# Attention steps reordered to scores, transposes, filler, transposes, values, with each head's maximum and exponentials as steps of their own

## The reference

```python
# layer 0: neighbourhood attention, 8 heads of 64, one row of the grid
s_lat = einsum('bhqd,bhiwd->bhqiw', q_r, k_blk) * scale + bias      # NEG outside of the neighbourhood
s_ctx = einsum('bhqd,bhcd->bhqc', q_r, kc) * scale
p = softmax(concatenate([s_lat, s_ctx]))
out = p_lat @ v_blk + p_ctx @ vc
# layer 1: sliding-window attention, 8 heads of 64, window 128, context keys and a sink logit per head
p = softmax(concatenate([s_lat, s_ctx, s_sink]))
out = p[..., :span] @ v_w + p[..., span:span + n_ctx] @ vc
# both: out = merge(out) * silu(gate projection)
```

## Time and profile before

| | |
|---|---|
| median of 3 runs | 1734.81 us (1733.99 to 1734.95) |
| the profiled execution | 1734.62 us |
| its span, first to last instruction | 1732.7 us |
| mean granted TensorE clock | 0.976 of 2.4 GHz |
| TensorE (PE) busy | 1624.4 us, 94% |
| VectorE (DVE) / ScalarE (ACT) / GpSimd (POOL) busy | 671.8 / 549.1 / 36.8 us |
| attention of layer 0 | about 335 to 790 us |
| attention of layer 1 | about 1380 to 1592 us |

### The profile page before, as it was taken

One profiled execution on the slowest core, in us unless ns is written; L12 is line 12 of the kernel. 1 busy time (PEld: TensorE's weight loads), 2 busy tenths in 40 slices (PEclk: granted clock), 3 DMA queues, 4 the chain that ended last, 5 costly groups with the idle time before them and its releaser, 6 DMA issues.

```text
span 1732.7 us, 25988 instructions
## 1 busy us (share of the span) xinstructions
PE 1624.4 (94%) x10106; PEld 1028.6 (59%) x10106; DVE 671.8 (39%) x1529; ACT 549.1 (32%) x1256; POOL 36.8 (2%) x108
## 2 busy tenths in 40 slices
PE   6999999899999999889999899999899799999996
PEld 4666866556565556544747665675564355555484
DVE  2123444413323214321255624244445265554165
ACT  0232242323323224432022332124214365554023
POOL 0000000000000000000000000000000011111000
PEclk9999999899999999999999998999999899999997
DMA  9100021112123113000545411000001000001353
GB/s 382 55 25 25 1 98 62 61 61 105 43 73 122 50 37 123 25 13 28 183 144 164 161 49 49 13 25 26 13 1 49 25 13 1 25 14 43 107 174 115
DMA packets 41144, 120.63 MB, mean 70 GB/s; under 512 B 4288, under 2 KB 14784, under 8 KB 39744
## 3 DMA queue, kind: packets, MB, share of 16 engines
q1 hardware_dynamic: 41024, 118.97, 19.6%
HBM read 109.52 MB, written 9.44 MB: 69 GB/s over the span
## 4 chain that ended last, share of the span: by engine, by line
PE 72%; issue 16%; DVE 6%; ACT 3%; DMA 1%; POOL 0%; SPq 0%; DVEq 0%; ACTq 0%; POOLq 0%
PE proj L986 22%; PE mixed L986 12%; PE scores L986 5%; PE proj L970 4%; PE mixed L970 3%; PE mixed L1106 3%; PE turned L1092 3%; PE scores L1204 2%; PE scores L1072 2%; PE scores L1232 2%; PE scores L1075 1%; ACT vstage L1669 1%; PE turned L1243 1%; PE mixed L931 1%; ACT yT L1669 1%
## 5 line engine op out<-in xcount | busy, mean ns | idle before, releaser
L986 PE MATMUL proj<-hT,weights 128*128 128x512 f32 (+1 forms) x1280 | 519.5, 552 | 10.3 <-DVE yT L1354 3.6
L986 PEld LDWEIGHTS proj<-hT,weights 128*128 128x128 f32 x1280 | 237.3, 194 | 219.3 <-issue 208.6
L986 PE MATMUL mixed<-hT,weights 128*128 128x512 f32 (+1 forms) x336 | 143.5, 571 | 0.8 <-ACT pair L1669 0.8
L986 PE MATMUL mixed<-yT,weights 128*128 128x256 f32 (+1 forms) x432 | 122.7, 442 | 0.0
L1669 ACT ACTIVATE work<-work,stat 128x640 f32<-128x640 f32 (+8 forms) x144 | 108.8, 755 | 42.6 <-DVE stat L1413 38.8
L1512 DVE SCALAR_TENSOR_TENSOR work<-work,turned 128x128 f32<-128x128 f32 (+1 forms) x152 | 53.0, 349 | 141.5 <-PE turned L1243 138.3
L1669 ACT ACTIVATE work<-turned 128x512 f32<-128x512 f32 (+2 forms) x136 | 72.7, 535 | 109.4 <-PE turned L1088 98.5
L1092 PEld LDWEIGHTS turned<-consts,work 128*128 128x128 f32 (+4 forms) x656 | 75.4, 140 | 53.4 <-issue 34.1
L1092 PE MATMUL turned<-consts,work 128*128 128x128 f32 (+4 forms) x656 | 100.4, 281 | 7.0 <-ACT work L1669 7.0
L986 PEld LDWEIGHTS mixed<-yT,weights 128*128 128x128 f32 x432 | 82.1, 190 | 38.9 <-issue 31.1
L986 PEld LDWEIGHTS mixed<-hT,weights 128*128 128x128 f32 x336 | 62.6, 191 | 63.4 <-issue 61.5
(11 more groups left out here) (249 smaller groups left out, 2124.3 us busy)
## 6 DMA issues: line engine op xcount, KB each, us to landing
weights<-in_weights SPq DMA_DIRECT2D x138, 512.0 KB, 3.6
tables<-in_bias SPq DMA_DIRECT2D x8, 1281.0 KB, 7.1
hT<-in_xT SPq DMA_DIRECT2D x8, 640.0 KB, 16.0
yT<-in_weights SPq DMA_DIRECT2D x8, 512.0 KB, 8.5
work<-in_xT SPq DMA_DIRECT2D x24, 128.0 KB, 3.6
x1T<-yT SPq DMA_DIRECT2D x12, 256.0 KB, 2.2
work<-in_weights SPq DMA_DIRECT2D x4, 512.0 KB, 16.4
pair<-in_weights SPq DMA_DIRECT2D x4, 512.0 KB, 17.4
```

Of the source, the lines that this page charges most:

```text
L986: last = nc.tensor.matmul(PJ[BANK_OF[u]][:, 0:n], weights[:, w % WBUFS, k, :], src[:, k, t0:t0 + n], start=(k == 0), stop=(k == KT - 1))
```

## The change

Each attention step now starts with the scores of unit x + 2; then groups 0 and 1 of the transposes of unit x; then, for head 0 of unit x + 2, the maximum (`top`, VectorE) and the exponentials (`exp`, ScalarE); then a gap marker; then the other group of transposes; then `top` and `exp` for head 1; then the values of unit x - 1. With the marker in the list, both weavers put filler in only at the gaps, so one place in each step (the parts of `interleave` that do so are as before, those of `alternate` are new). The instructions, their sizes and the semaphores they wait for are otherwise the same.

```diff
--- before.py
+++ after.py
@@ -182,10 +182,12 @@
             units[-1].append(s)
         else:
             units.append([s])
-    slots, passed, done, out = sum(s[0] != "softmax" for s in main), 0, 0, []
+    marked = any(s[0] == "gap" for s in main)
+    slots, passed, done, out = sum(not marked or s[0] == "gap" for s in main), 0, 0, []
     for s in main:
-        out.append(s)
-        passed += s[0] != "softmax"
+        if s[0] != "gap":
+            out.append(s)
+        passed += not marked or s[0] == "gap"
         while done < passed * len(units) // slots:
             out += units[done]
             done += 1
@@ -255,12 +257,15 @@
     for x in range(-2, n + 1):
         step = []
         turns = [("ptrans", *named(x), g) for g in range(len(turn_groups(named(x)[1])))] if 0 <= x < n else []
+        new = named(x + 2) if x + 2 < n else None
+        if new:
+            step.append(("scores", *new))
         step += turns[:2]
-        if x + 2 < n:
-            step.append(("scores", *named(x + 2)))
-        step += turns[2:]
-        if x + 2 < n:
-            step.append(("softmax", *named(x + 2)))
+        if new:
+            step += [("top", *new, 0), ("exp", *new, 0)]
+        step += [("gap",)] + turns[2:]
+        if new:
+            step += [("top", *new, 1), ("exp", *new, 1)]
         if 0 <= x - 1 < n:
             step.append(("pv", *named(x - 1)))
         steps.append(step)
@@ -1397,22 +1402,21 @@
                                    PJ[BANK_OF[u]][:, 0:n * P]),
                      ("proj_free", u), *([("filled", "na", j, "v")] if 4 * g + 4 >= VG else []))
 
-            def s_softmax(uid, unit):
+            def s_top(uid, unit, hh):
                 _, l, j, i = uid
                 st = stat[:, i % 4, :]
                 dve.wait_ge(*at(("scores", uid)))
                 lo, n = unit_cols(unit)
-                for hh in range(2):
-                    if before(uid, 2):
-                        dve.wait_ge(*at(("turned", before(uid, 2), turned_by(before(uid, 2), hh))))
-                    if l == 0 and i == 0:
-                        dve.wait_ge(*at(("bias", j, hh)))
-                    table = (const("band") if l or unit.box is None else
-                             tables[:, hh * BIAS:(hh + 1) * BIAS])[:, unit.bias:unit.bias + n]
-                    least = col("sink_neg", j + 4 * hh) if l else HIGHEST
-                    link(V.tensor_tensor_reduce(prob[i % 2][hh][:, 0:n], score_bank[hh][:, lo:lo + n], table, -1.0,
-                                                least, ALU.add, ALU.min, st[:, hh:hh + 1]),
-                         ("softmax_max", uid, hh), *([("softmax_dve", uid)] if hh else []))
+                if before(uid, 2):
+                    dve.wait_ge(*at(("turned", before(uid, 2), turned_by(before(uid, 2), hh))))
+                if l == 0 and i == 0:
+                    dve.wait_ge(*at(("bias", j, hh)))
+                table = (const("band") if l or unit.box is None else
+                         tables[:, hh * BIAS:(hh + 1) * BIAS])[:, unit.bias:unit.bias + n]
+                least = col("sink_neg", j + 4 * hh) if l else HIGHEST
+                link(V.tensor_tensor_reduce(prob[i % 2][hh][:, 0:n], score_bank[hh][:, lo:lo + n], table, -1.0,
+                                            least, ALU.add, ALU.min, st[:, hh:hh + 1]),
+                     ("softmax_max", uid, hh), *([("softmax_dve", uid)] if hh else []))
 
             def s_ptrans(uid, unit, g):
                 _, l, j, i = uid
@@ -1649,7 +1653,7 @@
 
             part = {"setup": s_setup, "ada": s_ada, "ada_turn": s_ada_turn,
                     "modulate": s_modulate, "mm": s_mm,
-                    "rope": s_rope, "vgather": s_vgather, "softmax": s_softmax, "ptrans": s_ptrans, "pv": s_pv,
+                    "rope": s_rope, "vgather": s_vgather, "top": s_top, "ptrans": s_ptrans, "pv": s_pv,
                     "gate0": s_gate0, "lin_scale": s_lin_scale, "lin_mul": s_lin_mul,
                     "lin_attend": s_lin_attend, "lin_chunk": s_lin_chunk, "lin_out": s_lin_out, "lin_norm": s_lin_norm, "rows": s_rows,
                     "centre": s_centre, "square_sum": s_square_sum, "scale": s_scale, "blend": s_blend, "next": s_next}
@@ -1762,16 +1766,15 @@
                     run(dst, ps, ACT.Copy, [("proj_free", u)] + ([("filled", *kind)] if t0 + n == T else []),
                         scale=QSCALE if scaled else 1.0)
 
-            def s_softmax(uid, unit):
+            def s_exp(uid, unit, hh):
                 _, l, j, i = uid
                 st, (_, n) = stat[:, i % 4, :], unit_cols(unit)
-                for hh in range(2):
-                    act.wait_ge(*at(("softmax_max", uid, hh)))
-                    if l:
-                        run(st[:, 4 + hh:5 + hh], col("sink", j + 4 * hh), ACT.Exp, bias=st[:, hh:hh + 1])
-                    pr = prob[i % 2][hh][:, 0:n]
-                    run(pr, pr, ACT.Exp, [("softmax_act", uid, hh)], scale=-1.0, bias=st[:, hh:hh + 1],
-                        accum_out=st[:, 2 + hh:3 + hh])
+                act.wait_ge(*at(("softmax_max", uid, hh)))
+                if l:
+                    run(st[:, 4 + hh:5 + hh], col("sink", j + 4 * hh), ACT.Exp, bias=st[:, hh:hh + 1])
+                pr = prob[i % 2][hh][:, 0:n]
+                run(pr, pr, ACT.Exp, [("softmax_act", uid, hh)], scale=-1.0, bias=st[:, hh:hh + 1],
+                    accum_out=st[:, 2 + hh:3 + hh])
 
             def s_ptrans(uid, unit, g):
                 if g % 2:
@@ -1885,7 +1888,7 @@
                 run(yT[:, f, t0:t0 + n], hT[:, f, t0:t0 + n], ACT.Identity, [("x_after", l, ci, f)],
                     bias=col("ln_b", l * 8 + f))
 
-            part = {"setup": s_setup, "early_copy": s_early_copy, "mm": s_mm, "gates": s_gates, "gates_sum": s_gates_sum, "softmax": s_softmax, "ptrans": s_ptrans,
+            part = {"setup": s_setup, "early_copy": s_early_copy, "mm": s_mm, "gates": s_gates, "gates_sum": s_gates_sum, "exp": s_exp, "ptrans": s_ptrans,
                     "gate0": s_gate0, "lin_scale": s_lin_scale, "lin_square": s_lin_square, "lin_turn": s_lin_turn,
                     "rows": s_rows, "rows_exp": s_rows_exp, "rows_turn": s_rows_turn,
                     "centre": s_centre, "rstd": s_rstd, "scale": s_scale}
```

## The result

The changed kernel takes **1814.55 us** (median of 4 runs, 1811.15 to 1818.19), the kernel before 1734.40 us in the same measurement (4 runs, 1732.90 to 1734.95). The ratio is **1.0457**, 95% interval 1.0443 to 1.0472: 80 us slower. The forecast was 1811 us. In one execution of a later experiment (the one gap behind the second maximum) the mean granted clock was 0.648 and the time 2452.95 us; it is left out of that experiment's numbers.

What follows compares the result with a forecast made beforehand. TensorE, busy 94% of the span, was taken to bound the kernel. Layer 0's 83.2 plus layer 1's 25.3, less 37.8 gained, plus 6 for the clock gave +76.7 us: 1811 us, range 1768 to 1850.

Steps and rivals of the forecast that it cites:

- The bound and what the change takes away: TensorE's idle time in both layers' attention: at most 37.8 us can be gained, all counted as removed.
- First part, handoffs: Layer 0: 36 places where filler units follow each other directly and wait for the one PSUM bank, 42.4 us.
- Second part, gate units: Layer 0: gate units ahead of the second maximum delay the next scores; sum with related waits 38.7 us.
- Third part, layer 1: Layer 1's attention: waits around single mm filler steps, ropes, gate units and empty gaps, 25.3 us.
- rope pairs: Layer 1: gaps holding the last mm and its rope, 2.8 us for each pair.
- empty gaps: Layer 1, x = 25 to 31: every second gap has no filler, 3.6 us.
- rope waits 0.9 for ScalarE's copy: Layer 1, rope directly behind the last mm: TensorE waits 0.9 us for ScalarE's copy.
- Fourth part, the clock: Idle time at three places (x = 9, 10) lowers the granted clock: 6 us, bounds 0 and 15.
- The gates cost no more than now: Rival, both layers: gate waits stay near today's, some 35 us fall away, about 1772 us; chance 0.14.
- Faster: Rival, at the gaps: all 37.8 us go and new waits come to less, 1716 us; chance 0.04.
- nothing: Rival, in the weavers: filler could still be spread, leaving the time at 1735 us; chance 0.02.
- The clock swings: Rival, vgather steps and context joins: clock falls in some 12 places, 36 to 60 us more, about 1850; chance 0.10.

Runs made afterwards that it cites:

- the run with spread filler and held gates: Changed kernel's step order without gap marker, filler spread as before, both VectorE products of gate units issued behind the second maximum: 1766.65 us, ratio 1.0179.
- the run with the gates held: Changed kernel, with VectorE's two products of each gate unit within attention issued behind the step's second maximum: 1763.87 us, ratio 1.0168.
- the run with only the second product held: Changed kernel, with only VectorE's second product of each gate unit within attention moved behind the second maximum: 1781.63 us, ratio 1.0262.
- order alone: New order of the step without the gap marker, filler handed out over the main steps as in the kernel before: 1787.99 us, ratio 1.0306.
- gap alone: Kernel before with its old step order, plus the gap marker between the scores and the last group of transposes: 1819.50 us, ratio 1.0482.
- two gaps: Changed kernel with a second gap in each step, behind the second maximum and its exponentials: 1762.13 us, ratio 1.0157.
- before, second product held: Kernel before, with only the second VectorE product of gate units moved behind the maxima of the step: 1722.60 us, ratio 0.9929.

## Why the prediction was right, point by point

**The bound and what the change takes away.** Right in the main: TensorE's waits for the sums and for ScalarE's copies in layer 0 fell from 12.6 to 3.3 us. They were a small part, as the bound of 37.8 us said. In layer 1 the transposes still wait 2.2 us for ScalarE (2.5 before).

**First part, handoffs.** Predicted 42.4 us in 36 places, with 1.1 in the last gate units and 0.5 for the weights of k; measured 36.7 us of projections waiting and 1.4 for weights. The mechanism held in each kind: 0.61 us behind a 256-column copy (0.7 predicted), 1.74 behind v (1.9), 1.59 to 1.98 for a vgather that opens a gap (2.0), 1.78 for the ada_turn (1.95). The prices were each a little high; part of it is that I counted from the next start of TensorE and the table counts from the modelled end of the last matmul. That TensorE waits in these places is shown by the trace. Their price in time is not: no run gave the projections a second bank, and the run with spread filler and held gates had 24.6 us less of such waits than the one with the one gap and was no faster.

**Second part, gate units.** Predicted 24.2 + 8.9 + 0.65 and 1.6 us of scores' waits in layer 0, 35.4 together; measured 34.4. The single waits at x = 9 and 10 were forecast as 3.4 and 3.0 and came out as 3.18 and 2.85. Its cost in time was shown by the run with the gates held to be some 50 us in both layers, more than its waits: the prediction had this cost, but gave the clock's share of it too little (see the fourth part).

**Third part, layer 1.** The term was too small: predicted 25.3 - 9.5 = 15.8 us more idle, measured 22.8. Scores' waits for the maximum were about right: 16.2 us, against 14.5 in the terms of the rope pairs and gate units and up to 3.6 in those of the empty gaps. The term that failed is "rope waits 0.9 for ScalarE's copy". It waits 1.9 us on average, four times:

```profile
1456.93 0.83 ACT L1673 ACTIVATE work<-work,stat 128x640 f32<-128x640 f32 x1
...
1457.88 0.60 ACT L1673 ACTIVATE vstage<-proj 128x512 f32<-128x512 f32 x1
...
1458.63 1.46 PE L1037 MATMUL proj<-vstage,consts 128*128 128x512 f32 x2 [2.12 <-ACT vstage L1673]
```

When the last `mm` of 1.8 us is over, ScalarE has the exponentials of head 0 still ahead of it in its queue (the long one starts at 1456.93); it copies at 1457.88, and the rope has idled for 2.12 us. I had counted that queue for VectorE in layer 0 but not for ScalarE here. Another 2.3 us are the first scores of the last stage waiting for the last output of attention, which I had not seen.

**Fourth part, the clock.** The right effect, mis-sized: predicted 6 us in a range of 0 to 15, while TensorE's busy time grew by 14.0 us in the two stages, 13.2 in layer 0. A small-unit stretch, and those around the gate unit shown above, columns as before:

```profile
425.00:430.00 5.00, 5.00 (x39) 3.91 (x38) 1.97 (x5) 1.40 (x3) 0.30 (x1) 0.66 0.00 0
...
460.00:465.00 5.00, 3.95 (x16) 1.56 (x14) 0.69 (x1) 1.49 (x3) 0.00 (x0) 1.00 0.00 0
465.00:470.00 5.00, 2.87 (x11) 1.75 (x12) 1.94 (x5) 1.34 (x3) 0.29 (x1) 0.60 0.00 2
470.00:475.00 5.00, 5.00 (x15) 2.79 (x14) 1.48 (x3) 1.48 (x3) 0.00 (x0) 0.72 0.00 0
475.00:480.00 5.00, 4.91 (x21) 2.30 (x19) 0.19 (x1) 0.89 (x2) 0.00 (x0) 1.00 0.00 0
```

After the wait of 3.18 us that ends at 467.13 the granted clock stands at 0.60 and 0.72, that is at its lower level for most of the time, while scores and transposes run at half their pace (the eight transposes at 469.42 take 1.94 us, against 1.08 in the earlier trace rows). The Trainium skill's rule ("TensorE: Matmul & The Clock Gate", section "A second HAM failure mode: psum-queue depth-cycling") says that short idle moments from waiting on PSUM make the clock swing. By that rule, the trace agrees in kind: the clock also stood at 0.66 from 425 to 430 us, among small vgather units, where no wait is over 2 us. In size the loss is 14 us, not the rival's 36 to 60.

Most of the loss went with the gate units' waits and not with the handoffs. In the run with the gates held the projections of layer 0 still wait 36.7 us, and in the run with only the second product held 37.0 us; TensorE was busy for 1620.2 and 1618.2 us there, 16 to 18 us less than in the changed kernel.

**The errors cancelled.** Between the two stages and the forecast: layer 0 had 7.2 us less idle time than forecast (83.2 - 28.4 = 54.8 against 47.6), layer 1 7.0 us more, and the clock took 8 us more. The stretches outside of the two stages took 2.4 us less. Together that leaves the profiled execution 5.3 us above the sum, and the median 3.5 us. That the total came so close is luck: the terms were off by up to 8 us, in both directions. The growth lies where it was forecast: from the second maximum of x = 10 to that of x = 20 (20 units and three gate units) the kernel took 116.8 us before and 136.6 after, while from that of x = 30 to the end of the stage it took 109.3 before and 101.3 after.

**The rivals.** "The gates cost no more than now" is refuted by 34.4 us of scores' waits in layer 0 and by the run with the gates held. (Its sum is not quite right: 1811 less some 35 is 1776, not 1772.) "Faster" and "nothing" are refuted by the time. "The clock swings" asked for 36 us or more and got 14.

## What to carry to other kernels

When work is interleaved on several in-order engines, price the place of each filler unit on every queue: what its reader has ahead of it when the unit ends, and which later instruction of the critical loop stands behind it. Concentrating filler at one point hides the waits there but exposes the handoff of a single buffer between consecutive units, and a consumer chain that spans two engines holds up everything behind it. Test two such changes together and not only one by one: here 52 and 84 us apart made 80 together. Of such a chain, keep in place the part that frees the shared buffer and move only the rest behind the step that others wait for; here that was worth 0.7% on the kernel that was already the faster one.

## What the runs showed of the hardware that was not expected

More idle time on TensorE lowered the granted clock in some orders and not in others. One profiled execution of each, in us:

| | idle | busy | mean granted clock |
|---|---|---|---|
| before | 108.3 | 1624.4 | 0.976 |
| order alone | 140.4 | 1646.1 | 0.965 |
| gap alone | 165.0 | 1654.1 | 0.965 |
| changed kernel | 178.5 | 1636.3 | 0.968 |
| changed, second product held | 157.3 | 1618.2 | 0.981 |
| changed, both products held | 142.5 | 1620.2 | 0.979 |
| two gaps | 139.9 | 1617.7 | 0.982 |
| before, second product held | 101.9 | 1615.2 | 0.982 |

The order alone and the two gaps are idle for the same time, yet one is busy for 28.4 us longer on the same matmuls. So the sum of the idle time does not give the clock's share. What sets it is not shown; the mean granted clock rose from 0.968 to 0.981 and 0.979 when the gate units' products no longer stood ahead of the second maximum.
